# Dense attention scores in two full passes and two 32-row tiles, with the hi and lo parts made at the up projections

## The reference

```
h = rmsnorm(x);  proj = h @ w_in                    # columns: qa ka va ga | cq ckv kr gb
ya = window_attention(qa, ka, va, sink) * silu(ga)  # 8 heads, |t-s| <= 128
q  = rmsnorm(cq)  @ w_uq                            # 8 heads x (64 nope + 32 rope)
kv = rmsnorm(ckv) @ w_ukv                           # 8 heads x (64 k_nope + 64 v)
s  = (q_nope . k_nope + rope(q_rope) . rope(kr)) * 96**-0.5     # kr is one for all heads
yb = softmax(s) @ v * silu(gb)                      # dense, all 1024 keys
out = rmsnorm(x + concat(ya, yb) @ w_out)
```

## Time and profile before

| | us |
|---|---|
| median of three runs | 655.42 |
| the profiled execution's own time | 655.55 |
| its span | 653.8 |
| up projections on PE | 95.3 to 144.5 |
| dense attention on PE, first units | 347.9 to 369.1 |
| dense attention on PE, units with all their parts | 369.1 to 552.6 |
| after the last scores | 552.6 to 653.8 |

### The profile page before, as it was taken

The page is one execution under the profiler, slowest core; times in us unless marked ns, Lnnn a source line. Parts: engine busy times, 40 slices in busy tenths (PEclk is TensorE's granted clock), DMA queues, the critical chain, the costliest instruction groups (busy, mean ns, idle before and its releaser), DMA issues.

```text
span 653.8 us, 8923 instructions
## 1 busy us (share of the span) xinstructions
PE 632.7 (97%) x3252; PEld 536.6 (82%) x3252; DVE 407.8 (62%) x773; ACT 331.8 (51%) x717; POOL 302.1 (46%) x283
## 2 busy tenths in 40 slices
PE   3999999999999999999999999999999999999996
PEld 3899998888888878888878788888888887888884
DVE  4863326334221158999985988888888888955422
ACT  4542222213222147777774877777777778404312
POOL 4962004402323244363545776876786777820000
PEclk9999999999999999999999999999999999999998
DMA  7730006363121210100122101011013201403521
GB/s 238 232 123 0 1 29 240 142 250 101 34 65 33 64 34 1 32 2 1 48 99 73 40 2 42 12 30 41 1 42 102 100 1 34 161 1 125 181 81 65
DMA packets 31612, 47.38 MB, mean 72 GB/s; under 512 B 2544, under 2 KB 19440, under 8 KB 31440
## 3 DMA queue, kind: packets, MB, share of 16 engines
q1 hardware_dynamic: 31568, 46.81, 22.6%
HBM read 35.13 MB, written 11.67 MB: 72 GB/s over the span
## 4 chain that ended last, share of the span: by engine, by line
PE 91%; DVE 3%; ACT 2%; issue 1%; DMA 1%; POOL 1%; SPq 0%; ACTq 0%; DVEq 0%; POOLq 0%
PE ps L1099 21%; PE ps L1101 21%; PE ps L1100 21%; PE ps L1308 8%; PE ps L1324 4%; PE ps L1325 4%; PE ps L1241 2%; PE ps L1251 2%; PE ps L1252 1%; PE ps L1230 1%; PE ps L1229 1%; DMA g_mix<-norm_mix 1%; PE ps L1111 1%; PE ps L1133 1%; DVE x_n L831 1%
## 5 line engine op out<-in xcount | busy, mean ns | idle before, releaser
L523 POOL TENSOR_SCALAR p_b<-p_b,stat 128x1024 f32<-128x1024 f32 x64 | 71.9, 1123 | 52.9 <-DVE stat L1023 52.2
L738 ACT ACTIVATE pT_hi<-ps 128x512 fp32r<-128x512 f32 x128 | 69.9, 596 | 38.5 <-PE ps L1308 38.4
L1018 DVE TENSOR_REDUCE stat<-ps 128x1 f32<-128x1024 f32 x64 | 77.7, 1213 | 10.2 <-PE ps L1101 10.1
L1099 PE MATMUL ps<-hT_hi,w_hi 128*128 128x512 f32 x208 | 83.7, 402 | 0.0
L1028 DVE TENSOR_TENSOR pT_lo<-ps,pT_hi 128x512 fp32r<-128x512 f32 x128 | 81.8, 680 | 1.4 <-ACT pT_hi L738 1.4
L1101 PE MATMUL ps<-hT_hi,w_lo 128*128 128x512 f32 x208 | 81.3, 391 | 0.0
L1100 PE MATMUL ps<-hT_lo,w_hi 128*128 128x512 f32 x208 | 81.0, 390 | 0.0
L729 ACT ACTIVATE p_b<-ps,stat 128x1024 f32<-128x1024 f32 x64 | 71.5, 1118 | 12.0 <-DVE stat L1018 11.7
L1308 PEld LDWEIGHTS ps<-ident,p_b 128*128 128x128 f32 x512 | 59.3, 141 | 12.1 <-issue 2.6
L1308 PE MATMUL ps<-ident,p_b 128*128 128x128 f32 x512 | 67.3, 273 | 1.0 <-DVE pT_lo L1028 0.9
L406 POOL TENSOR_SCALAR w_hi<-w_raw 128x1024 fp32r<-128x1024 f32 x13 | 14.1, 1081 | 91.4 <-PE ps L1101 91.4
(11 more groups left out here) (155 smaller groups left out, 1433.1 us busy)
## 6 DMA issues: line engine op xcount, KB each, us to landing
w_raw<-w_in SPq DMA_DIRECT2D x13, 512.0 KB, 3.9
x_in<-x SPq DMA_DIRECT2D x8, 512.0 KB, 3.7
wo_raw<-w_out SPq DMA_DIRECT2D x8, 512.0 KB, 4.4
x_r<-x SPq DMA_DIRECT2D x8, 512.0 KB, 3.7
out<-o_n SPq DMA_DIRECT2D x16, 256.0 KB, 2.4
q_nope_scratch<-stage SPq DMA_DIRECT2D x8, 256.0 KB, 2.8
k_nope_scratch<-stage SPq DMA_DIRECT2D x8, 256.0 KB, 2.1
v_scratch<-stage SPq DMA_DIRECT2D x8, 256.0 KB, 2.0
```

Source lines behind the costliest of these rows:

```text
L523: nc.gpsimd.tensor_scalar(p_b[:, (U + 1) % 4, :], p_b[:, (U + 1) % 4, :], r_b[:, U % 4:U % 4 + 1], 0.5, ALU.mult, ALU.mult).then_inc(s_bp, 1)
L738: nc.scalar.activation(pT_hi[:, G % 2, 4 * a:4 * a + 4, U % 4 * P:(U % 4 + 1) * P], ps[:, 4 + a, :].rearrange("p (k c) -> p k c", c=P), AC ...
L1018: nc.vector.tensor_reduce(nm_b[:, U % 4:U % 4 + 1], ps[:, b:b + 2, :].rearrange("p b c -> p (b c)"), AX.X, ALU.max, negate=True).then_inc( ...
L1099: nc.tensor.matmul(o, a_hi, b_hi, start=first, stop=False)
```

## The change

Every q, k and v is split right where it leaves PSUM. ACT writes hi into `st_hi` (4 slots), DVE then writes lo = PSUM - hi into `st_lo` (q with the scale in one instruction); for the rotated part DVE rotates in place in `r_tmp`, ACT copies hi, DVE subtracts. SP stores hi and lo of each job, 60 stores. All 30 jobs now pass through both engines, and the bank is free when lo is written.

In the dense attention the loads bring finished hi and lo rows into tiles made up for the new scores. With n for the 64 nope rows and r for the 32 rope rows:

- pass A, 128 rows: qa = [q_n_hi; q_r_hi; q_r_lo], ka = [k_n_hi; k_r_hi; k_r_hi]
- pass B, 128 rows: qb = [q_n_hi; q_n_lo], kb = [k_n_lo; k_n_hi]
- the remaining q_r_hi * k_r_lo, 32 rows: qc holds q_r_hi twice (rows 0 to 31 and 32 to 63), kc holds k_r_lo of keys 0 to 511 in rows 0 to 31 and of keys 512 to 1023 in rows 32 to 63. The two 32-row matmuls of a unit use different rows of the array and write different PSUM banks.

So a unit has four 128-row matmuls and two of 32 rows in place of six of 96 rows. All splitting of q, k and v by POOL, ACT and DVE in and just before the dense attention is gone. Per head SP issues 14 loads for q and k (before: 4) and 2 for v (before: one for all heads). `load_v(h)` waits for the products of head h-2, and stands ahead of the `wo_raw` loads. Tiles move in SBUF, and three `wo_hi` tiles with them.

```diff
+            def wait_slot(eng, j):      # j >= 4: both stores of job j-4 have landed
+                    eng.wait_ge(s_st[j % 4], 32 * (j // 4))
...
@@ block.sync @@
             for j, (kind, t, h) in enumerate(UP):
-                wait_up_copied(sp, j)
...
-                sp.dma_start(dst, src).then_inc(s_st[j % 4], 16)
+                sp.wait_ge(s_uph, j + 1)
+                sp.dma_start(dst[0], hi).then_inc(s_st[j % 4], 16)
+                sp.wait_ge(s_upl, j + 1)
+                sp.dma_start(dst[1], lo).then_inc(s_st[j % 4], 16)
...
+            def load_qa(h):
+                i, rows = h % 2, slice(h * HD, (h + 1) * HD)
+                sp.dma_start(f(qa[i][0:HD, :]), qh_scr[rows, :]).then_inc(s_qk[i], 16)
+                load_rope(qa[i], HD, qrh_scr, h)
+                load_rope(qa[i], QK, qrl_scr, h)
+                sp.dma_start(f(ka[i][0:HD, :]), kh_scr[rows, :]).then_inc(s_qk[i], 16)
+
+            def load_qb(h):
+                i, rows = h % 2, slice(h * HD, (h + 1) * HD)
+                for tile, p0, scr in ((qb, 0, qh_scr), (qb, HD, ql_scr), (kb, 0, kl_scr), (kb, HD, kh_scr)):
+                    sp.dma_start(f(tile[i][p0:p0 + HD, :]), scr[rows, :]).then_inc(s_qk[i], 16)
+                for r in range(2):
+                    load_rope(qc[i], ROPE * r, qrh_scr, h)
...
+            load_qa(0)
+            load_k_rope(0)
             sp.wait_ge(s_ws, REP * W_UNITS)
-            sp.dma_start(v_raw[:, :, :], v_scr.rearrange("(t p) c -> p t c", p=P)).then_inc(s_vr, 16)
-            for h in range(1, HEADS):
-                load_qk(h)
+            sp.wait_ge(s_wm, REP * W_UNITS)
+            load_qb(0)
+            load_qa(1)
+            load_k_rope(1)
+            load_qb(1)
+            sp.wait_ge(s_g, 2 * NM)
+            load_v(0)
+            load_v(1)
+            for h in range(2, HEADS):
+                sp.wait_ge(s_bs, NT * (h - 1))
+                load_qa(h)
+                load_qb(h)
+                sp.wait_ge(s_bpv, 2 * (h - 1))
+                load_v(h)
@@ block.gpsimd @@
-                if U // NT + 1 < HEADS:
-                    split_piece(U // NT + 1, U % NT)
...
@@ block.scalar @@
             for j, (kind, t, h) in enumerate(UP):
+                if kind == "r":
+                    if t == 1:
+                        act.wait_ge(s_rot, h + 1)
+                        for i in (j - 1, j):
+                            wait_slot(act, i)
+                            last = nc.scalar.activation(st_hi[:, i % 4, :], r_tmp[:, 2 * (i - j + 1), :], ACT.Copy)
+                        last.then_inc(s_uph, 2)
                     continue
                 act.wait_ge(s_up, j + 1)
+                wait_slot(act, j)
+                nc.scalar.activation(st_hi[0:n, j % 4, :], ps[0:n, UP_BANK[j % 8], :], ACT.Copy,
+                                     scale=B_SCALE if kind == "q" else 1.0).then_inc(s_uph, 1)
...
@@ block.vector @@
+                    nc.vector.tensor_tensor(r_tmp[:, 0, :], r_tmp[:, 0, :], r_tmp[:, 1, :], ALU.subtract)
+                    nc.vector.tensor_tensor(r_tmp[:, 2, :], r_tmp[:, 2, :], r_tmp[:, 3, :],
+                                            ALU.add).then_inc(s_rot, 1)
+                    dve.wait_ge(s_uph, j + 1)
+                    for i in (j - 1, j):
+                        last = nc.vector.tensor_tensor(st_lo[i % 4][:, :], r_tmp[:, 2 * (i - j + 1), :],
+                                                       f(st_hi[:, i % 4, :]), ALU.subtract)
+                    last.then_inc(s_upl, 2)
...
+                dve.wait_ge(s_uph, j + 1)
+                    last = nc.vector.tensor_tensor(lo, src, f(hi), ALU.subtract)
+                last.then_inc(s_upl, 1)
...
@@ block.tensor, scores_b @@
                 for c in range(2):
-                    k = slice(c * HALF, (c + 1) * HALF)
-                    last = three(ps[:, 2 * (U % 2) + c, :], q_hi[:, hp, q], q_lo[:, hp, q], k_hi[:, hp, k],
-                                 k_lo[:, hp, k], True, True)
+                    k, o = slice(c * HALF, (c + 1) * HALF), ps[:, 2 * (U % 2) + c, :]
+                    nc.tensor.matmul(o, qa[i][:, q], ka[i][:, k], start=True, stop=False)
+                    nc.tensor.matmul(o, qb[i][:, q], kb[i][:, k], start=False, stop=False)
+                for c in range(2):
+                    r = slice(ROPE * c, ROPE * (c + 1))
+                    last = nc.tensor.matmul(ps[:, 2 * (U % 2) + c, :], qc[i][r, q], kc[r, :], start=False, stop=True)
                 last.then_inc(s_bs, 1)
```

More of the change, by code:

```diff
@@ L119, in encoder @@
         uv_lo = at("uv_lo", 85, [P, KVLT, HEADS, HD], F32R)
-        stage = at("stage", 89, [P, 4, HALF])
+        st_hi = at("st_hi", 89, [P, 4, HALF], F32R)
+        st_lo = [at(f"st_lo{i}", kb, [P, HALF], F32R) for i, kb in enumerate((113, 142.5, 144.5, 205))]
         r_tmp = at("r_tmp", 97, [P, 4, HALF])
@@ L205, in encoder @@
             "w_transposed", "w_pT_hi", "w_pT_lo", "w_pv", "w_o_lo", "w_o", "w_y"))
-        s_h0, s_h0l = sem("head0_hi"), sem("head0_split")
-        s_vr, s_krl, s_qki = sem("v_raw_in"), sem("k_rope_in"), sem("qk_raw_in")
-        s_sph, s_sph2, s_sp, s_sp2 = sem("qk_hi_split"), sem("v_hi_split"), sem("qk_split"), sem("v_split")
+        s_qk = [sem(f"qk_in{i}") for i in range(2)]
+        s_v = [sem(f"v_in{i}") for i in range(2)]
         s_bs, s_bm, s_be, s_br, s_bp = (sem(n) for n in (
@@ L233, in wait_up_copied @@
         def wait_up_copied(eng, j):
[L235 to L239, removed]
+            eng.wait_ge(s_upl, j + 1)
         def wait_all_stored(eng):
             for i in range(4):
-                eng.wait_ge(s_st[i], 16 * len(range(i, len(UP), 4)))
+                eng.wait_ge(s_st[i], 32 * len(range(i, len(UP), 4)))
+        def wait_slot(eng, j):
+            if j >= 4:
+                eng.wait_ge(s_st[j % 4], 32 * (j // 4))
         M_COLS = [KA] + [QA + P * i for i in range(4)] + [GA + P * i for i in range(4)] \
@@ L345, in _, with load_v @@
+            def load_v(h):
+                i, cols = h % 2, slice(h * HD, (h + 1) * HD)
+                for scr, c in ((vh_scr, 0), (vl_scr, HD)):
+                    sp.dma_start(f(vB[:, i, :, c:c + HD]),
+                                 scr[:, cols].rearrange("(t p) c -> p t c", p=P)).then_inc(s_v[i], 16)
             wait_all_stored(sp)
+            for r in range(2):
+                sp.dma_start(f(kc[ROPE * r:ROPE * (r + 1), :]),
+                             krl_scr[:, r * HALF:(r + 1) * HALF]).then_inc(s_qk[0], 16)
@@ L706, in _ @@
                     exp_w(s, 0)
-                else:
-                    head0_hi()
                 for i, c in enumerate(keys[:2]):
@@ L881, in _ @@
             for j, (kind, t, h) in enumerate(UP):
-                if kind == "r" and t == 1:
+                n = ROPE if kind == "kr" else P
+                src, hi, lo = ps[0:n, UP_BANK[j % 8], :], st_hi[0:n, j % 4, :], st_lo[j % 4][0:n, :]
+                if kind == "r":
+                    if t == 0:
+                        continue
                     x1, x2 = ps[:, UP_BANK[(j - 1) % 8], :], ps[:, UP_BANK[j % 8], :]
```

161 lines of the change are left out of this document (50 added, 111 removed).

## The result

The changed kernel takes 673.05 us (median; 672.15 to 673.58) against 655.47 us for the kernel before on the same chip: ratio 1.0266, 95% interval 1.025 to 1.0282. It is 17.6 us slower. The forecast was 649.9 us with a range of 642 to 662: wrong in sign and size.

What follows compares the result with a forecast made beforehand. PE, busy 97% of the span, was taken to bound the kernel. Terms -13.4 + 5.9 - 1.3 + 0.4 - 0.2 + 3.0 gave -5.6 us from 655.55, so 649.9 us, range 642 to 662.

Steps and rivals of the forecast that it cites:

- Scores: Dense attention: the 32-row pair costs 0.23 us, one full pass, gaining 0.232 us in each of 58 units: -13.4 us.
- rival 3: Dense attention: PE empties itself at each change between full and 32-row work; pair 0.55 us, kernel 663.2 us; chance 0.14.
- -13.4 + 5.9 - 1.3 + 0.4 = -8.4: Dense attention terms in us: shorter scores, transposes late behind DVE, shorter first units, lead lost in the last two units.
- What DVE gives back: Dense attention: every fourth unit, transposes wait for `pT_lo`, 0.42 us in each of 14 groups: +5.9 us.
- Up projections, the rotation: Second half of the up projections: PE waits 2.3 us for banks until DVE's subtraction; part of +3.0 us (0 to 6).
- Up projections, the tail of the stores: After the up projections: first gated projections copied out only when all is stored, about +0.7 us, within the +3.0.
- Handoff: Start of dense attention: head 0's eight loads land near 347.1, just hidden before PE's scores: -0.2 us (-0.5 to +1).
- Output weights, POOL: Late `wo_raw` loads arrive in time for the output stage, and dropping POOL's splits gains nothing: 0 us each.

Runs made afterwards that it cites:

- five full passes: Changed kernel with the pair of 32-row matmuls replaced by one full 128-row matmul, one score term left out: 658.93 us.
- ACT's wait moved: Changed kernel with ACT waiting for all stores at its ninth gated copy instead of its first: 666.69 us.
- one tile: Changed kernel with the second 32-row matmul of each unit left out: 672.86 us.
- six full passes: Changed kernel with the pair of 32-row matmuls replaced by two full 128-row matmuls, one score term left out: 665.88 us.
- 64 rows: Changed kernel with the pair of matmuls given 64 rows each instead of 32, from the pass B tiles: 673.28 us.
- the pair twice: Changed kernel with the pair of 32-row matmuls issued twice in each unit: 686.85 us.
- no lo stores: Changed kernel with SP storing only hi, and the loads of lo reading hi: 665.32 us.
- three waits mended and six full passes: Changed kernel with ACT's store wait, SP's head 0 loads and POOL's gated weight splits moved, and two 128-row matmuls for the pair: 656.18 us.

## Why the prediction was wrong

- **Scores, the step that failed.** "I take 0.23, since the loads fit and the two tiles share neither rows nor PSUM bank." The tiles do overlap, and both loads are in within 0.18 us. But they don't go ahead of the change of form, and the way in and out adds 0.29 us to the 0.23, plus 0.05 in the transposes: unit 3.29 instead of 2.96. That is rival 3, which had 0.55 for the pair and 3.28 for the unit, and 0.14 of the chances. Its size was right in sum and not in its parts: it put 0.16 on each way, and the runs have 0.09 and 0.20 + 0.05. Its argument against ("PE passes from 96-row scores to 128-row transposes at the plain distance") didn't bear on the question. It stands that 96 to 128 rows costs nothing; 64 and 32 rows cost the same 0.29. The Trainium skill had the rule (TensorEngine Tiling (Array Packing), "Key Properties": a change of tiling mode drains the engine). The trace of after agrees, 0.09 us in and 0.20 out. The Trainium skill also has tiles about 4 ns apart and loads pulled ahead (TensorE: Matmul & The Clock Gate, "Part 3: Packing small matmuls"). The first fits the two and the four tiles inside one row of 0.50 or 0.51 us; the second didn't occur at the border between the forms. The dense attention changed by 64 units at 3.29 less 3.19, 6.4 us, less about 1 at its two ends: +5.5, against the -13.4 + 5.9 - 1.3 + 0.4 = -8.4 forecast. Of the 23.7 us between the forecast and the profiled 673.58 us, 13.9 are here.
- **What DVE gives back.** It didn't come up, since no unit was short enough. With five full passes it did, at (13.4 - 7.9) / 14 = 0.39 us per group by the same account, against 0.42, and through the wait that was forecast: the transposes start 0.82 us after `pT_lo`.
- **Up projections, the rotation.** PE idled 1.9 us, ended by DVE's subtraction, against 2.3. Right in place and size. With POOL's weight splits moved to after job 20 the stall is gone.
- **Up projections, the tail of the stores.** Sized at 0.7 us, it cost 5.7 and 1.8 of slow clock. The forecast saw that the backlog of the rotation would hardly shrink, and took bytes over the best rate (1.30 us per job). The drain did go at 1.32 to 1.35 us per v job (ACT's copies start at 147.56, 148.88, 150.19, 151.54), each after 0.7 us of waiting for a slot, whose stores land 3.3 to 3.7 us after issue (2.3 or 2.4 for the rotated rows). But PE's last up projection was over at 147.3, ACT's copy of the last job started only at 154.1, after 2.0 us of waiting for its slot, DVE's at 154.75, and the last landing, at 159.2, came 3.7 us after its issue. The sizing left out both, the late last copy and the landing behind it. ACT, waiting for that landing, held the gated banks. With ACT's wait moved 6.4 us come back. The range of 0 to 6 was too narrow for 2.8 + 5.8 + 1.8 = 10.4 in all, against +3.0: 7.4 of the 23.7.
- **Handoff.** "Just hidden", -0.2, bounds to +1. It was 1.3 late. SP needed 4.4 us for the eight loads (351.51 to 355.9), 4.2 were priced. But the last piece of `qc` was issued at 355.47 and took 4.9 us, where the forecast had 3.4, and PE started only at 360.48. The `qc` pieces have the median 5.0 in the changed kernel. Pieces of the same 64 KB for `qa` have 3.2 and 2.8; these follow one load of 256 KB and not four, which is the likely reason, though no run was made for it. 1.5 of the 23.7.
- **Output weights, POOL.** 0, as forecast: the output stage is 97.0 us against 97.1.

The rest of the 23.7 is the 1.0 us of the start. Had the pair been priced as rival 3 and the tail as measured, the sum would have been near 671 us. One sum of the prediction doesn't come out of its own terms: with all its bounds bad (give-back of all 13.4, 6 for the up projections, +1 and +0.8) the forecast's range ends at 662 and not at 656. What stays open: after the 1.9 us of idle time at the rotation the clock fell to 0.50 in the traces of one tile, six full passes, ACT's wait moved, 64 rows and the pair twice, which cost 1.0 us of the up projections (52.2 or 52.3 us instead of 51.2), and stayed at 1.00 in those of the changed kernel, five full passes and no lo stores; no run was made for that.

## What to carry to other kernels

Two tiles in separate row groups run at the price of one and four at the price of two, but PE pays some 0.3 us each time it goes into that form and back, more than one 512-column pass. So a leftover product of a few rows is worth packing only if its pieces are gathered, as many as banks allow, into one entry: a single pair costs 0.57 us against 0.46 for two full passes and loses, four tiles cost the same 0.57, waits aside, against 0.92 for four. The gathered tiles need their banks earlier, and the wait for these took back part of the gain here. When stores are doubled, ask for the landing of the last one and who waits for it, not for bytes over the best rate, and put a wait for all stores where the waiting engine has nothing urgent behind it.

## What the runs showed of the hardware that was not expected

- The cost of entering and leaving is the same for 32 and 64 rows (673.05 and 673.28 us) and for one, two and four tiles (0.50 or 0.51 us recorded each time); a second round inside costs 0.22 us.
- The clock fell to 0.50 after a single idle time of 5.7 us and stayed there for 3.9 us of full work; in the version with 0.3 us of idle time at that place it didn't fall. After 1.9 us of idle time, at the rotation, it fell in five traces of eight.
- Splitting hi and lo at the source moved 68.4 MB instead of 46.8 through the DMA queue, and yet with its three waits mended and six full passes it took the same time as before (ratio 1.0001): the added traffic was hidden but for two small waits, and the dense attention, without its splits, was 1.5 us shorter. The two cancel.
- DVE's subtraction and addition of 128x512 took 0.92 and 1.52 us while POOL split weights, and 0.69 and 0.68 beside an idle POOL.
